# Moving two dense tiles of a delta head from one stage's head to another stage's tail

## The chip, the cores and the metric

One program runs on one core of a Trainium2 chip. The metric is the device time of one execution in microseconds (us), lower is better. The core has five engines with queues of their own: TensorE (PE; its weight loads are shown apart as PEld), VectorE (DVE), ScalarE (ACT), GpSimd (POOL) and SyncE (SP, which here only starts transfers).

## What is computed

Three blocks of a language model on 512 tokens of width 1024, in fp32. The change lies in the first, a mix of a state space part (Mamba-2) and a gated delta rule part:

```python
h = rmsnorm(x, norm_mix_w)
proj = h @ w_in
(ssm_z, ssm_xbc, ssm_dt, gdn_qkv, gdn_z, gdn_a, gdn_b, gate_ssm, gate_gdn) = split(proj)
y_ssm = mamba2_mixer(ssm_z, ssm_xbc, ssm_dt, ...)   # conv, chunked scan, * silu(z), norm
y_gdn = gdn_mixer(gdn_qkv, gdn_z, gdn_a, gdn_b, ...) # conv + silu, 8 heads, delta scan
merged = sigmoid(gate_ssm) * (y_ssm @ w_proj_ssm) + sigmoid(gate_gdn) * (y_gdn @ w_proj_gdn)
x = x + merged @ w_out
```

In `gdn_mixer` the 3072 columns of `gdn_qkv` pass a causal depthwise convolution of four taps and a silu, and are then query, key and value of eight heads of width 128. Each head normalises query and key, solves a unit triangular system in each chunk and runs a scan over chunks.

## The kernel before, in words

**Dense tiles.** Every weight matrix is cut into tiles of 128 output columns. A tile with eight blocks of 128 input rows is computed in four pieces (`("dense", name, j, c)`, two blocks each). A block takes three matmuls of 128x128 by 128x512 (L1054, L1055, L1056), since each fp32 number is split in two rounded parts; a tile is thus 24 matmuls. SP fetches the tile's weights (a panel, 512 KB) into one of three buffers W, ScalarE rounds them into one of four buffers R (L2518), GpSimd forms the rest in four steps (L2910). These `split` steps stand on every engine's queue two panels ahead of the tile that uses them. Two PSUM banks take turns for dense tiles.

**Queues.** Each engine runs its list strictly in order and waits on semaphores. The lists come from `order()`, at build time. Two calls of its planner `weave` matter here: one for the state space stage, one for the delta stage. `weave` gets chains of steps and lists of dense tiles ("fills"), and follows four engines in time with given durations per step (`SEG`). A chain step that is ready goes first; TensorE takes a piece of a dense tile when no chain step is ready, and the next tile as soon as what it depends on (`room`, `AFTER`) and its bank are free. On the other engines steps are ranked by the length of what follows them, and steps that empty a dense bank (`conv`, `sz`, `gate` and others) get 40 us on top. The delta stage is planned for itself, behind the last step of the state space stage on each queue.

**State space stage, tail.** Per group F of 128 columns: dense tile s_z F, then `sz` (ScalarE L2623, VectorE L1882), `sy` (TensorE L1187 and L1190, VectorE L1888 and L1891). After the last four F comes a normalisation: `sn1` (ScalarE square, L2627), `sn1p` (TensorE sums, L1065), `sn2` (VectorE, a root by small steps), `sn2p` (TensorE spreads it, L1072), `sn3` (four VectorE multiplications, L1906) and `pair` (ScalarE L2548 and VectorE L1720 split the result in two parts).

**Delta stage.** g_qkv is tiled so that channel j of the convolution `("conv", "qkv", j)` reads g_qkv tile 8 (j mod 3) + j div 3: head h has channels 3h, 3h+1, 3h+2. `conv` is one ScalarE step (L2564) and three VectorE steps (L1764); `conv2` is ScalarE L2571 and VectorE L1771. Head 2 keeps its channels in tiles 59, 60 and 61 of SBUF, and the same tiles hold masks and the z product of the state space stage until its last F. Two chains run, heads 0, 2, 4, 6 and heads 1, 3, 5, 7. A head begins with `hq` (eight transposes, L1088), which for head 0 waits for the last `sn3`, because it transposes into the bank (4) that `sn3` reads:

```python
w.wait_ge(*CV.dve.at("out", "qkv", 3 * h + 1))
if h == 0:
    w.wait_ge(*SS.dve.at("yn", 7))
transpose4(bank[q.Y], t(q.k)).then_inc(*GD.pe.up("kt", h))
```

Then come `hg` (a row product L1084, VectorE L1969), `hn` (normalisation, ends with L1960), `hnp` (transposes), `hn2` (ScalarE L2658), `hb` (VectorE L1979), `hu` (L1094), an inversion (`i0`, `il`, `ix`, `ip`, `it`, `iq`, `im`, `iu`, `in_`: L1102 or corners L1208 on TensorE, L2637 on ScalarE, L1926 or L1944 on VectorE), a scan over four chunks (`hs1` to `hs3`), and an end with dense tile g_z. The fills are first the remaining g_qkv tiles, a head's three tiles waiting for the head three before it, and then gate_s, p_ssm (eight each), gate_g (eight) and p_gdn (eight half tiles, which need heads 0 to 3 done). In the order before, a pair of heads covers twelve such tiles, the last pair ten; the last four p_gdn half tiles stand between the steps of head 7's inversion.

Of the kernel before, what the change touches and what calls it, by code (L numbers as in the profile page):

```python
# [192 lines left out]
XORD = (8, 9, 10, 11, 0, 1, 2, 3, 4, 5, 6, 7)  # L193
# [75 lines left out]
for f in range(3):  # L269
    PAIR[f"hid{f}"] = (tuple(FS[j % 4] for j in range(NFF)), tuple(range(16, 60, 2)), tuple(range(17, 60, 2)))  # L270
FFN = (("ff_in", 0, "ff_in", 22, 1), ("f1g", 0, "f1u", 0, 4), ("f2g", 0, "f2u", 0, 6))
CONV = {
    "xbc": ("ssm_conv_w", XS, 12, lambda j: ("s_xbc", j), lambda j: ("xbc", XORD[XORD.index(j) - 2]) if XORD.index(j) >= 2 else None),
    "qkv": ("gdn_conv_w", tuple(x for h in range(8) for x in QKV[h % 3]), 24, lambda j: ("g_qkv", 8 * (j % 3) + j // 3),
            lambda j: ("qkv", j - 2) if j >= 2 else ("xbc", 6 + j)),
}
# [6 lines left out]
def rm_bank(q, hh, i):  # L283
# [8 lines left out]
    pair="s.63 v.75", hq="p.86", hqs="s1.2", hn="v6.9", hnp="p.43", hn2="s.6", hg="p.23 v1.38 s1.23", hb="p.23 v1.5",  # L292
# [16 lines left out]
def tiles(name, j, *after):  # L309
    return [("dense", name, j, c) for c in range(-(-WTS[name][1] // CH))] + list(after)  # L310


def opens(name, j):
# [47 lines left out]
    "sa": lambda qb, *u: [("sc", m, qb - 1) + u for m in range(2 if u[0] == "d" else 1)] if qb else [("an3",) + u] + [("fr", u[1]), ("frq", u[1])] * (u[0] == "f"),  # L361
    "sb": lambda m, qb, *u: [("sa", qb) + u],
    "sc": lambda m, qb, *u: [("sb", m, qb) + u], "sd": lambda qb, *u: [("sc", m, qb) + u for m in range(2 if u[0] == "d" else 1)],
    "conv": lambda which, j: [("conv2",) + CONV[which][4](j)] if CONV[which][4](j) else [],
    "conv2": lambda which, j: [("conv", which, j)], "branch": lambda name, j, gname, gj, x, m: [("gate", gname, gj, x)],
    "part": lambda name, j, gname, gj, x, m: [("gate", gname, gj, x)],
    "do_": lambda f: [("dg", f), ("sd", 3, "d", f)], "ft1": lambda h: [("sd", 3, "f", h)],
# [29 lines left out]
def room(name, j):  # L397

    if name == "s_z":
        return [("sy", j - 1)] if j else []  # L400
    if name == "g_z":
        return [("hs3", j, 3)]
    if name == "pa" and j >= 13:
        return [("s3", j - 13, 7)]
    if name == "g_qkv":
        return [("ho2", j % 8 - 3)] if j % 8 >= 3 else []
    if name == "pa":
        return [("pair", "yr", j % 4 - 2)] if j < 12 and j % 4 >= 2 else []
    if name == "gm" and j >= 8:
        return [("ry3", 2)] if j >= 12 else [("ixs", 3, 7)]  # L410
    if name == "a_out":
        return [("pair", "yr", p) for p in range(4)]
    if name == "qkv2":
        return [("pair", "yr", j % 4 + 2)] if j % 4 < 2 else [("ry3", 2), ("ry3", 3), ("branch", "a_out", 7, "gm", 7, M2[7], None)]
    if name == "gb":
        return [("pair", "yr", j + 2)] if j < 2 else [("do_", j - 2)]
    if name == "p_gdn":
        return [("pair", "ygdn", h) for h in range(4)]
    if name == "b_out":
        return [("pair", "yd", p) for p in range(2)]  # L420
    if name == "b_proj":
        return [("pair", "ydiff", h) for h in range(6)]
    if name == "a_proj":
        return [("pair", "yg", f) for f in range(4)]
    if name == "in3" and 16 <= j < 20:
        return [("gn2", 3)] + ([("pair", "yg", j - 18)] if j >= 18 else [])
    if name == "in3" and j >= 24:
        return [("ft3", j % 8 - 4)] if j % 8 >= 4 else [("pair", "yg", 3)] if j % 8 >= 2 else []
    return []


def weave(chains, *fills):
# [9 lines left out]
    for c in units:  # L442
        before = None
        for u in c:
            for k, s in enumerate(u):
                wants[s] = room(*s[1:3]) if s[0] == "dense" and s[3] == 0 else [u[k - 1]] if k else after(s, before)
            before = u[-1]
    for f in dense:
        for u in f:
            for s in u:  # L450
                if s[0] == "dense":
                    wants[s] = room(*s[1:3]) if s[3] == 0 else []
                else:
                    wants[s] = [[x for x in u if x[0] == "dense"][-1]] + (AFTER[s[0]](*s[1:]) if s[0] in AFTER else [])
# [146 lines left out]
def convs(which, js):  # L601
    out = []
    for n, j in enumerate(js):
        out += tiles(*CONV[which][3](j), ("conv", which, j))
        if n:
            out.append(("conv2", which, js[n - 1]))
    return out + [("conv2", which, js[-1])]
# [12 lines left out]
def gdn_head(h):  # L620
    out = [("hq", h), ("hqs", h), ("hg", h), ("hn", h), ("hnp", h), ("hn2", h), ("hb", h), ("hu", h)]
    out += inversion(("g", h), 3) + [("hk", h)]
    for c in range(4):
        out += ([("hs1", h, c)] if c else []) + [("hs2", h, c), ("hs3", h, c), ("ho", h, c)]
    return out + [("hon", h), tiles("g_z", h, ("hz", h)), ("hos", h), ("ho2", h)]
# [72 lines left out]
def gated(name, gname, g0, x, m=None, gates=True):  # L698
    out = []
    for j in range(8):  # L700
        if gates:
            out += tiles(gname, g0 + j, ("gate", gname, g0 + j, x[j]))
        out += tiles(name, j, ("branch", name, j, gname, g0 + j, x[j], m and m[j]))
    return out
# [15 lines left out]
def order():  # L720
    O = [("begin",), ("ada0",), ("halves",)]
# [6 lines left out]
    def channel(g):  # L728
        out = []
        for F in range(4 * g, 4 * g + 4):  # L730
            after = [(k, F + 1, hh) for k in ("ch", "che") for hh in range(2)] if F % 4 < 3 else []
            out += ([(k, F, hh) for k in ("ch", "che") for hh in range(2)] if F % 4 == 0 else []) + [("cm", F, 0), ("cm", F, 1), tiles("s_z", F, ("sz", F))]
            out += after + [("sy", F)] + ([("xd", F + 4)] if g == 0 else [])
        return out

    def normed(g):
        out = []
        for f in range(4):
            out += [("sn1", g, f), ("sn1p", g, f)]
        return (out + [("sn2", g), ("sn2p", g)] + [("sn3", 4 * g + f) for f in range(4)]  # L740
                + [("pair", "yssm", 4 * g + f) for f in range(4)])

    chain = [tiles("small", 0)] + [("sums", n) for n in range(5)]
    for g in range(2):
# [1 line left out]
        for c in range(3):  # L746
            chain += [("st0", g, c), ("st", g, c)]
        chain += channel(g)
    O += weave([chain, normed(0) + normed(1)], convs("xbc", XORD) + convs("qkv", range(6)))

    rest = gated("p_ssm", "gate_s", 0, M1)
    rest += [s for j in range(8) for s in tiles("gate_g", j, ("gate", "gate_g", j, GG[j]))]
    rest += [s for j in range(8) for s in tiles("p_gdn", j, ("part", "p_gdn", j, "gate_g", j, GG[j], M1[j]))]
    heads = [[s for h in range(a, 8, 2) for s in gdn_head(h)] for a in range(2)]
    O += weave(heads + [[("pair", "ygdn", h) for h in range(4)]], sum([convs("qkv", range(3 * h, 3 * h + 3)) for h in range(2, 8)], []), rest)
    O += [("pair", "ygdn2", h) for h in range(4)]
    O += wide(followed("p_gdn2", "gate_g", 0, GG, M1, "m1") + residual("w_out", 1))
    O += ffn(0, "ff_dn", 2, True)
# [11 lines left out]
    rest = [s for j in range(8) for s in tiles("gm", j, ("gate", "gm", j, M2[j]))] + sum(gates[:4], [])  # L770
# [19 lines left out]
    rest = gated("a_proj", "in3", 0, M3) + gates  # L790
# [77 lines left out]


ORDER = [x if x[0] in ALONE else (ALL, x) for x in order()]  # L870
ON_PE = [s for e, s in ORDER if "p" in e]
TURN = turns(ON_PE)
# [2272 lines left out]
```

## Time and profile before

| | |
|---|---|
| time, median of 3 runs | 3094.06 us (3093.57 to 3095.58) |
| profiled execution, from first to last instruction | 3089.4 us |
| time around that span (median less span) | 4.7 us |
| TensorE busy | 2977.7 us, 96% |
| VectorE, ScalarE, GpSimd busy | 1605.5, 1078.7, 1412.1 us |
| state space stage's last `sy` ends on TensorE | 234.06 us |
| delta stage on TensorE | 246.47 to 724.48 us |
| granted TensorE clock, mean | 0.988 |

The profile shows one execution. Times in its rows are microseconds from the start of the span, durations in us, and "PE" before a line number is TensorE's matmul row. A wait is written as idle time of an engine with the instruction that ended it. `PEclk`, in the rows of stretches the third number from the end, is the clock that was granted to TensorE, 1.00 for 2.4 GHz and 0.50 for 1.2 GHz. The execution's own time is not shown apart from the span, so the time around it is taken from the median.

### The profile page before, as it was taken

Reading aid. Unit: us, or ns where it says so; the run is one execution under the profiler, and the core shown is the slowest. Engines: PE = TensorE matmul, PEld = TensorE weight load, DVE = VectorE, ACT = ScalarE, POOL = GpSimd, SP = SyncE. Lnnn points to the kernel's source line nnn. Section 1 sums busy time; section 2 is a strip of 40 time slices with the busy share of each in tenths; the row PEclk is TensorE's granted clock in tenths of the full one; section 3 lists DMA queues with packets and bytes.
Section 4 is the critical chain, followed back from the end, with each engine's and each line's share of the span. In section 5 each row is a group of like instructions: output and inputs, shape, how many; then the busy total and the mean of one; then the engine's idle time right before and its main releaser. Section 6 shows DMA issues by size and latency. Waiting matters only on the chain.

```text
span 3089.4 us, 42486 instructions
## 1 busy us (share of the span) xinstructions
PE 2977.7 (96%) x16912; PEld 2385.2 (77%) x16912; DVE 1605.5 (52%) x3295; ACT 1078.7 (35%) x1781; POOL 1412.1 (46%) x1817
## 2 busy tenths in 40 slices
PE   6998999999999999999999999999899999999999
PEld 5777777787888887767877778888776768788887
DVE  5766567566566416559744453330466773433310
ACT  4443333333322223323324433222354553332221
POOL 3553344344556544314334364555543334655554
PEclk9999999999999999999999999999999999999999
DMA  3211112112344432102112222333321112232232
GB/s 123 83 55 60 57 55 69 55 56 82 117 149 144 129 96 66 36 21 69 36 48 75 69 82 96 96 94 101 101 69 61 58 59 81 84 96 96 97 103 88
DMA packets 72358, 248.02 MB, mean 80 GB/s; under 512 B 8160, under 2 KB 8544, under 8 KB 72032
## 3 DMA queue, kind: packets, MB, share of 16 engines
q1 hardware_dynamic: 72160, 245.30, 24.8%
q8 instruction: 134, 2.20, 0.3%
q14 instruction: 64, 0.52, 0.1%
HBM read 243.18 MB, written 2.10 MB: 79 GB/s over the span
## 4 chain that ended last, share of the span: by engine, by line
PE 84%; DVE 12%; ACT 2%; issue 1%; POOL 1%; DMA 0%; SPq 0%; DVEq 0%; ACTq 0%; POOLq 0%
PE bank L1054 23%; PE bank L1056 22%; PE bank L1055 22%; PE bank L1088 3%; PE bank L1102 3%; PE bank L1533 1%; PE bank L1065 1%; PE bank L1551 1%; DVE sm L1617 1%; DVE sm L1619 1%; PE bank L1542 1%; PE bank L1372 1%; DVE sm L1621 1%; POOL t L2943 1%; DVE t L1764 1%
## 5 line engine op out<-in xcount | busy, mean ns | idle before, releaser
L2910 POOL TENSOR_TENSOR R<-W,R 128x256 fp32r<-128x256 f32 x1715 | 1287.9, 784 | 1540.5 <-ACT R L2518 1540.5
L1054 PE MATMUL bank<-u,R 128*128 128x512 f32 (+1 forms) x3440 | 1393.9, 405 | 27.2 <-DVE u L1720 8.3
L1056 PE MATMUL bank<-u,R 128*128 128x512 f32 (+1 forms) x3440 | 1348.8, 392 | 0.0
L1055 PE MATMUL bank<-u,R 128*128 128x512 f32 (+1 forms) x3440 | 1347.8, 392 | 0.0
L1054 PEld LDWEIGHTS bank<-u,R 128*128 128x128 f32 (+1 forms) x3440 | 649.2, 189 | 182.5 <-issue 15.9
L1056 PEld LDWEIGHTS bank<-u,R 128*128 128x128 f32 (+1 forms) x3440 | 648.6, 189 | 142.4 <-issue 0.4
L1055 PEld LDWEIGHTS bank<-u,R 128*128 128x128 f32 (+1 forms) x3440 | 650.3, 189 | 127.5 <-issue 4.8
L2518 ACT ACTIVATE R<-W 128x1024 fp32r<-128x1024 f32 (+2 forms) x454 | 452.3, 1002 | 143.3 <-PE bank L1056 136.8
L2548 ACT ACTIVATE u<-t 128x512 fp32r<-128x512 f32 x126 | 78.3, 630 | 322.9 <-DVE t L1742 249.1
L1753 DVE SCALAR_TENSOR_TENSOR X<-bank,X 128x512 f32<-128x512 f32 x32 | 22.1, 692 | 260.2 <-PE bank L1056 260.2
L1720 DVE TENSOR_TENSOR u<-t,u 128x512 fp32r<-128x512 f32 x126 | 97.3, 782 | 100.5 <-ACT u L2548 99.8
L1088 PE MATMUL bank<-CN,t 128*128 128x128 f32 x816 | 122.5, 281 | 20.5 <-DVE t L2044 5.4
L1728 DVE TENSOR_TENSOR t<-bank,t 128x512 f32<-128x512 f32 x66 | 45.5, 689 | 172.5 <-PE bank L1056 164.4
L1088 PEld LDWEIGHTS bank<-CN,t 128*128 128x128 f32 x816 | 91.5, 142 | 45.5 <-DVE t L2300 8.0
L2555 ACT ACTIVATE t<-t 128x512 f32<-128x512 f32 x66 | 41.7, 632 | 240.8 <-DVE t L1728 240.8
L1742 DVE TENSOR_TENSOR t<-t,bank 128x512 f32<-128x512 f32 x66 | 45.4, 688 | 128.2 <-PE bank L1056 126.3
L1102 PEld LDWEIGHTS bank<-t,t 64*64 64x64 f32 x2560 | 83.3, 134 | 30.6 <-issue 25.4
L1102 PE MATMUL bank<-t,t 64*64 64x64 f32 x2560 | 98.3, 222 | 0.1
L1764 DVE SCALAR_TENSOR_TENSOR t<-bank,sm,t 128x511 f32<-128x511 f32 (+2 forms) x108 | 80.6, 747 | 24.6 <-ACT t L2564 22.0
L2524 ACT ACTIVATE t<-X 128x512 f32<-128x512 f32 x48 | 29.8, 623 | 152.3 <-DVE X L1753 73.9
L2819 ACT ACTIVATE t<-t,sm 128x128 f32<-128x128 f32 (+3 forms) x96 | 62.0, 647 | 43.4 <-DVE sm L2318 42.8
L1733 DVE SCALAR_TENSOR_TENSOR t<-t,t 128x512 f32<-128x512 f32 x66 | 52.7, 798 | 37.7 <-ACT t L2555 37.7
(389 smaller groups left out, 2748.4 us busy)
## 6 DMA issues: line engine op xcount, KB each, us to landing
W<-in_in SPq DMA_DIRECT2D x48, 512.0 KB, 3.3
W<-in_ff_in SPq DMA_DIRECT2D x44, 512.0 KB, 3.3
W<-in_g_qkv SPq DMA_DIRECT2D x24, 512.0 KB, 3.3
W<-in_ada SPq DMA_DIRECT2D x24, 512.0 KB, 3.3
W<-in_f1g SPq DMA_DIRECT2D x22, 512.0 KB, 3.3
W<-in_f1u SPq DMA_DIRECT2D x22, 512.0 KB, 3.2
W<-in_f2g SPq DMA_DIRECT2D x22, 512.0 KB, 3.2
W<-in_f2u SPq DMA_DIRECT2D x22, 512.0 KB, 3.3
```

The source lines that it names most:

```text
L1054: e.matmul(b[0:cols, :], wh, hi, start=(k == 0), stop=False)
L1055: e.matmul(b[0:cols, :], wh, lo, start=False, stop=False)
L1056: i = e.matmul(b[0:cols, :], wl, hi, start=False, stop=(k == KT - 1))
L1088: i = e.transpose(b[:, m * 128:m * 128 + 128], x[:, m * 128:m * 128 + 128], C("ident"))
L1102: i = e.matmul(b[g, s], l[g, s], x[g, s], start=True, stop=True)
L1720: e.tensor_tensor(r(lo[k]), t(src[k]), r(hi[k]).bitcast(F32), SUB).then_inc(*PR.dve.up("lo", tag, k))
L1733: e.scalar_tensor_tensor(out=s, in0=t(FT[j % 2]), scalar=1.0, in1=s, op0=ADD, op1=MUL).then_inc(*FF.dve.up("s", f, j))
L1764: e.scalar_tensor_tensor(out=c[:, s:512], in0=b[:, 0:512 - s], scalar=half(wname, (3 - s) * nt + gj), in1=c[:, s:512], op0=MUL, op1=ADD).t ...
L2518: e.activation(R[q % NH][:, 0:n], W[p % NW][:, 0:n], ACT.Copy).then_inc(*PN.act.up("hi", key))
L2548: e.activation(r(hi[k]), t(src[k]), ACT.Copy).then_inc(*PR.act.up("hi", tag, k))
L2819: e.activation(ex, ex, ACT.Exp, bias=c[:, 0:1], scale=small[q.nw][:, 32 + 2 * qb + m:33 + 2 * qb + m], accum_out=c[:, 1:2]).then_inc(*AT.a ...
L2910: i = e.tensor_tensor(R[q % NH][:, 1024 + a:1024 + b], W[p % NW][:, a:b], R[q % NH][:, a:b].bitcast(F32), SUB)
```

## The change

Channels 6 and 7 of the qkv convolution, head 2's first two (g_qkv tiles 2 and 10), are planned in the state space stage's call of `weave` and no longer in the delta stage's. Two entries hold them back there: the two dense tiles depend on `sz` 7, the step that reads the last z tile's bank, and their `conv` steps on `sy` 7. Channel 8 stays in the delta stage, and everything that is computed stays as it is.

```diff
--- before.py
+++ after.py
@@ -361,7 +361,7 @@
     "sa": lambda qb, *u: [("sc", m, qb - 1) + u for m in range(2 if u[0] == "d" else 1)] if qb else [("an3",) + u] + [("fr", u[1]), ("frq", u[1])] * (u[0] == "f"),
     "sb": lambda m, qb, *u: [("sa", qb) + u],
     "sc": lambda m, qb, *u: [("sb", m, qb) + u], "sd": lambda qb, *u: [("sc", m, qb) + u for m in range(2 if u[0] == "d" else 1)],
-    "conv": lambda which, j: [("conv2",) + CONV[which][4](j)] if CONV[which][4](j) else [],
+    "conv": lambda which, j: [("sy", 7)] * (which == "qkv" and j in (6, 7)) + ([("conv2",) + CONV[which][4](j)] if CONV[which][4](j) else []),
     "conv2": lambda which, j: [("conv", which, j)], "branch": lambda name, j, gname, gj, x, m: [("gate", gname, gj, x)],
     "part": lambda name, j, gname, gj, x, m: [("gate", gname, gj, x)],
     "do_": lambda f: [("dg", f), ("sd", 3, "d", f)], "ft1": lambda h: [("sd", 3, "f", h)],
@@ -403,7 +403,7 @@
     if name == "pa" and j >= 13:
         return [("s3", j - 13, 7)]
     if name == "g_qkv":
-        return [("ho2", j % 8 - 3)] if j % 8 >= 3 else []
+        return [("ho2", j % 8 - 3)] if j % 8 >= 3 else [("sz", 7)] * (j in (2, 10))
     if name == "pa":
         return [("pair", "yr", j % 4 - 2)] if j < 12 and j % 4 >= 2 else []
     if name == "gm" and j >= 8:
@@ -746,13 +746,13 @@
         for c in range(3):
             chain += [("st0", g, c), ("st", g, c)]
         chain += channel(g)
-    O += weave([chain, normed(0) + normed(1)], convs("xbc", XORD) + convs("qkv", range(6)))
+    O += weave([chain, normed(0) + normed(1)], convs("xbc", XORD) + convs("qkv", range(8)))
 
     rest = gated("p_ssm", "gate_s", 0, M1)
     rest += [s for j in range(8) for s in tiles("gate_g", j, ("gate", "gate_g", j, GG[j]))]
     rest += [s for j in range(8) for s in tiles("p_gdn", j, ("part", "p_gdn", j, "gate_g", j, GG[j], M1[j]))]
     heads = [[s for h in range(a, 8, 2) for s in gdn_head(h)] for a in range(2)]
-    O += weave(heads + [[("pair", "ygdn", h) for h in range(4)]], sum([convs("qkv", range(3 * h, 3 * h + 3)) for h in range(2, 8)], []), rest)
+    O += weave(heads + [[("pair", "ygdn", h) for h in range(4)]], convs("qkv", range(8, 9)) + sum([convs("qkv", range(3 * h, 3 * h + 3)) for h in range(3, 8)], []), rest)
     O += [("pair", "ygdn2", h) for h in range(4)]
     O += wide(followed("p_gdn2", "gate_g", 0, GG, M1, "m1") + residual("w_out", 1))
     O += ffn(0, "ff_dn", 2, True)
```

## Rows read from the trace of the kernel before

**Rows 1.** The page: span, and busy time of each engine.

```profile
span 3089.4 us, 42486 instructions
...
PE 2977.7 (96%) x16912; PEld 2385.2 (77%) x16912; DVE 1605.5 (52%) x3295; ACT 1078.7 (35%) x1781; POOL 1412.1 (46%) x1817
```

**Rows 2.** Stretches, busy time by engine: start and end, length, then busy us (instructions), clock, DMA.

```profile
234.06:246.47 12.41, 3.02 (x17) 2.75 (x17) 7.98 (x25) 2.54 (x5) 0.00 (x0) 0.66 0.00 0
246.47:251.65 5.18, 5.18 (x17) 4.40 (x17) 1.43 (x3) 2.60 (x4) 2.79 (x4) 0.50 0.02 3
251.65:270.00 18.35, 17.78 (x88) 14.80 (x87) 16.26 (x32) 6.35 (x9) 9.39 (x13) 1.00 0.27 86
246.47:724.48 478.01, 463.51 (x3480) 376.23 (x3480) 305.97 (x648) 165.52 (x320) 191.69 (x236) 0.99 0.18 58
677.19:698.41 21.22, 21.22 (x214) 16.55 (x213) 13.27 (x25) 6.19 (x12) 11.89 (x14) 1.00 0.20 61
```

**Rows 3.** Chain that ended last, 228 to 252: start us, us, what.

```profile
228.50 0.23 PE bank L1055
...
232.15 0.23 PE bank L1056
...
234.10 0.76 DVE t L1888
...
236.29 1.07 PE bank L1065 x8
...
240.35 1.99 PE bank L1072 x8
242.36 0.76 DVE t L1906
...
246.47 1.97 PE bank L1088 x8
248.44 0.43 PE bank L1054
...
251.00 0.44 PE bank L1084
251.46 0.70 DVE t L1969
```

**Rows 4.** Timeline 225 to 300: start us, us, engine, line, operation [idle before, releaser].

```profile
226.96 1.04 ACT L2518 ACTIVATE R<-W 128x1024 fp32r<-128x1024 f32 x1
...
228.08 2.81 POOL L2910 TENSOR_TENSOR R<-W,R 128x256 fp32r<-128x256 f32 x4 [4.58 <-ACT R L2518]
```

**Rows 5.** Timeline 255 to 275, three engines.

```profile
255.77 0.69 ACT L2564 ACTIVATE t<-bank,sm 128x512 f32<-128x512 f32 x1 [0.79 <-PE bank L1056]
...
259.82 4.54 DVE L1764 SCALAR_TENSOR_TENSOR t<-bank,sm,t 128x511 f32<-128x511 f32 x6
...
261.81 0.59 ACT L2658 ACTIVATE t<-bank 128x512 f32<-128x512 f32 x1
...
262.19 0.50 PE L1054 MATMUL bank<-u,R 128*128 128x512 f32 x1 [0.57 <-DVE t L1764]
...
264.28 0.68 DVE L1979 TENSOR_TENSOR t<-t,bank 128x512 f32<-128x512 f32 x1
...
271.19 1.47 PE L1088 MATMUL bank<-CN,t 128*128 128x128 f32 x12
```

**Rows 6.** PE's waits in the delta stage: us in total, times, longest.

```profile
PE bank L1054 <- DVE t L1764: 3.6, 3, 1.5
```

**Rows 7.** Timeline, tail of the delta stage: one link, then PE's rows.

```profile
660.14 0.68 PE L1102 MATMUL bank<-t,t 64*64 64x64 f32 x16
...
660.87 0.69 DVE L1926 TENSOR_TENSOR t<-t,bank 128x512 f32<-128x512 f32 x1 [2.57 <-PE bank L1102]
...
679.39 0.51 PE L1102 MATMUL bank<-t,t 64*64 64x64 f32 x10
...
698.41 0.68 PE L1208 MATMUL bank<-t,t 64*64 64x64 f32 x8
```

## The prediction

> **What bounds the kernel now.** I read the page first: TensorE is busy 96% of the span, no other engine more than 52% [rows 1]. So a change in the order of the work can only win what TensorE idles, or what it does at a lower clock, at the place that the change touches. Next the stretches of time around that place [rows 2]. The state space stage ends its TensorE work on the last product (`sy` 7) at 234.06, and the delta stage's first instruction (`hq` 0, eight transposes) starts at 246.47. In these 12.41 us TensorE has 3.02 us of work, so 9.4 us are idle; the granted clock has sunk, and the next 5.18 us run wholly at 0.50, the 1.2 GHz level. The chain of waits says what the idle time is [rows 3]: VectorE combines `sy` 7, ScalarE squares, TensorE sums (L1065), VectorE takes a root from 237.4 to 240.3, TensorE spreads it (L1072), VectorE multiplies four tiles (L1906), and only then do the transposes get their turn, because `hq` 0 waits for the last of these four. Behind them in TensorE's queue stands tile 2 of g_qkv, which needs none of that.
>
> In the delta stage, 246.47 to 724.48, TensorE idles 478.0 - 463.5 = 14.5 us in all [rows 2], spread over many small waits, of which the convolution's L1764 causes 3.6 us in three [rows 6]. Here two chains of heads alternate with dense tiles that fill their waits.
>
> **What the edit moves.** g_qkv tiles 2 and 10 (query and key of head 2, channels 6 and 7 of the convolution) with their convolutions leave the head of the delta stage for the end of the state space stage, from 234.06 on. `sz` 7 ends on VectorE before `sy` 7 is combined at 234.10, so the hold costs TensorE nothing. No matmul, transfer or byte is added. The order of panels stays s_z 7, g_qkv 2, 10, 18, gate_s 0, so SP's queue only moves earlier. The panel of tile 10 is the one that GpSimd splits from 228.08 to 230.9 [rows 4], so both are ready at 234.06. The next splits (1.04 us on ScalarE, 2.8 on GpSimd each) have both engines free: GpSimd is idle in the whole gap [rows 2]. Cost of all this: nothing, covered by the gap; without cover one split would delay a later tile by up to 3.9 us.
>
> **Terms of the sum.**
> A. The two tiles. In the chain seventeen matmuls of a dense tile lie between 228.50 and 232.38, 0.228 us each [rows 3]. Two tiles are 2 x 24 x 0.228 = 10.9 us that the delta stage no longer holds.
> B. The clock. If the gap is filled, the transposes and the first dense work run at full clock. The eight transposes took 1.97 us [rows 3], twelve of them at full clock 1.47, so eight about 1.0 [rows 5]: 1.0 won. From 248.44 to 251.46 seven big matmuls take 0.43 each instead of 0.23 [rows 3], 1.4 won, and one more before the clock is back about 0.1. B = 2.5.
> C. Head 0 starts later. The two moved tiles now share TensorE with the tail's own two small jobs. Pieces of six matmuls (1.37 us) can't be interrupted: the sum L1065, ready at 236.29, starts after two pieces at 236.79, 0.5 late. The spread L1072, ready at about 240.85, starts behind the first piece of tile 10 at about 241.96, but takes 1.0 instead of 1.97, so it ends at 243.0, 0.7 later than now. Tile 2 is through at 240.6; ScalarE's first step takes 0.69 and VectorE's three steps about 2.3 (six take 4.54) [rows 5], 241.3 to 243.6, and an evacuation goes first in the planner's ranking, so I count it ahead of the four L1906. These, with two `pair` steps between them, took from 242.36 to the transposes' start at 246.47, 4.1 us [rows 3]; they now end at 247.7. TensorE's own queue is through with both tiles at 234.06 + 10.9 + 1.07 + 1.0 = 247.1, so VectorE decides: start at 247.7, C = -1.2. Its lower bound is 0.6 late (TensorE's queue alone), its upper bound, if the second convolution also stands ahead, is the rival below.
> D. New idle time. The planner gives dense tiles to TensorE as early as they fit, so the idle slots of the heads stay filled from the tiles behind (gate_s, p_ssm, gate_g), and what is missing is the last fill: four half tiles of p_gdn, eight pieces. They now run in the 21.2 us from 677.2 to 698.4, in which TensorE is wholly busy [rows 2], and between them stands head 7's inversion, from its third squaring at 679.39 to its last corner at 698.41, 19.0 us [rows 7]. One link there is a TensorE job of 0.68 and a VectorE step of 0.69, 660.14 to 661.56, so 1.42 [rows 7]. I count seven such links and a similar one over ScalarE: 11 us if nothing is in the way, 12 to 13 with head 6's jobs between. So without the eight pieces, 10.9 us, this stretch shrinks by only 6 to 7: 4 to 5 us of TensorE become idle. Lower bound 0: if the chains run faster earlier (next term), less fill is used there and more is left here. Upper bound 8, if only 3 us come out of the chain. I take 4.2, nearer to the counted links than to either end.
> E. VectorE is relieved in the head of the stage. It is busy 16.3 of 18.35 us there [rows 2], and head 0 waits behind six convolution steps, 259.82 to 264.36, before L1979 at 264.28; TensorE lost 0.57 at 262.19 for the same reason [rows 5]. These steps are gone from there. On TensorE that is 0.6 at least; I take 0.6, with up to 3 for the chain if the chain counts.
>
> Sum: 10.9 + 2.5 - 1.2 - 4.2 + 0.6 = 8.6 us less. The profiled span is 3089.4; the median of the runs, 3094.06, lies 4.7 above it, which is the time around the span and doesn't change. Span 3080.8, time **3085.5**, 0.28% less. What a measurement of this kernel can tell from no change is 0.2%, 6.2 us.
>
> Of the transposes the Trainium skill (TensorE: Matmul & The Clock Gate, Part 4: PE-mode transpose) says that the full clock doesn't engage for them. By it `hq` 0 would keep its 1.97 us, and the time would be 3086.5. The trace disagrees: twelve in 1.47 us.
>
> **Rivals.**
> 1. The heads' chain sets the delta stage, and fill taken from it is simply idle time. For it: links and pieces are planned to dovetail, and the stage's rounds end with head steps. Against it: only 14.5 of 478 us are idle, and TensorE's jobs there often stand behind a piece. What then counts is the chain of head 0: now its row product L1084 ends at 251.4; later 247.7 + 1.0 + 1.37 + 0.4 = 250.5, 0.9 sooner; and `hb` comes 1.8 sooner (L1979 starts at 264.28; the last step before it, L2658, ends at 262.4 [rows 5]). 2.7 us less: **3091.4**.
> 2. TensorE alone sets it: no new idle time, D = 0. Then 10.9 + 2.5 - 1.2 + 0.6 = 12.8 less: **3081.3**. For it: the 96%; against it: the last fill stands exactly where only two chains are left.
> 3. Slower: head 0 starts late and the stage is paced by its heads. If VectorE's queue has the second convolution ahead of the four L1906, it begins at 247.1 + 0.7 = 247.8, ends at 250.1, and the L1906 at 254.2; the transposes start 7.7 us later, TensorE idles 7 us before them, and as in today's gap the clock falls to 1.2 GHz, so B is lost as well. If the stage then keeps its 478 us, less the 1.8 us that `hb` wins, the time is 3094.1 + 7.7 - 1.8 = **3100.0**. Against it: by the planner's own order the four multiplications are ready (behind L1072) several us before tile 10's last matmul. It decides from a late start of about 5 us on, and only with the heads as the bound; with TensorE as the bound the same late start would still give 3094 or less.
> 4. The edit does not fill the gap, since the planner may put the tiles behind L1072: then nothing before 242 is filled, and the gain is that of rival 1 or less. It is counted there; the planner takes a known dense tile at the first free moment, so I think it unlikely.
>
> **How the numbers follow.** Forecast (6.2 to 11 us less) 0.49; rival 2 (11 to 14) 0.15; rival 1 with rival 4 (0 to 6 less) 0.28; rival 3 and other bad interleavings of a stage that is planned anew 0.08. Faster by over 0.2% is the first two, 0.64. Rival 1 and a small part of rival 3 are within 0.2%: 0.29. Slower: 0.07. The range reaches from rival 2's value with 0.8 for the bound of C, 3080.5, to the upper end of rival 1, 3094.0; outside lie rival 3 and the far ends, under 0.15. The likeliest case's own range is 3083 to 3088.
>
> **What would show it.** Right: the granted clock between 234 and 252 stays near 1.00; dense matmuls stand between 234.1 and 247; the transposes of `hq` 0 start at 247 to 248 and take 1.0 us; the first L1906 starts at 243 to 244. In round four (from about 600) idle time of 3 to 5 us appears before the scan of head 7, in the waits on L1926, L1944 or L2637. The distance from `hq` 0 to the stage's end falls from 478.0 to about 468. Wrong: that distance stays above 474 (rival 1), falls below 465 (rival 2), or the transposes start after 252 (rival 3). Most of all D is weak: it rests on which tiles the planner leaves for the end, and a new order may also cost waits in rounds two and three that nothing in the present trace shows.

## The result and the profile after

The changed kernel takes 3100.65 us (median of 12 executions, 3097.86 to 3115.65) against 3094.06 for the kernel before (12 executions beside it, 3092.99 to 3095.58). The ratio is 1.0029, 95% interval 1.0021 to 1.0037: slower by 0.29%, where 0.28% faster was forecast and 3080.5 to 3094.0 was the range.

The page after, span and busy time by engine, answers to [rows 1]:

```profile
span 3098.6 us, 42487 instructions
...
PE 2984.4 (96%) x16912; PEld 2389.3 (77%) x16912; DVE 1606.6 (52%) x3295; ACT 1077.8 (35%) x1781; POOL 1411.1 (46%) x1817
```

The stretches after, for [rows 2] (length, then busy us with instructions by engine, clock, DMA): from the end of `sy` 7 to `hq` 0, the half-rate part behind it, the delta stage, its last round, and a hole inside that round.

```profile
233.92:252.50 18.58, 13.04 (x64) 10.29 (x63) 14.90 (x32) 6.42 (x11) 5.87 (x8) 0.96 0.18 58
252.50:257.81 5.31, 5.30 (x17) 4.53 (x18) 2.67 (x5) 2.61 (x4) 3.37 (x4) 0.50 0.00 0
252.50:729.07 476.57, 455.63 (x3433) 368.27 (x3433) 301.93 (x642) 161.00 (x314) 185.52 (x228) 0.99 0.17 56
614.74:729.07 114.33, 103.66 (x801) 82.09 (x801) 81.20 (x172) 37.00 (x79) 35.80 (x42) 0.97 0.12 38
645.00:655.00 10.00, 5.11 (x40) 4.01 (x39) 8.29 (x25) 4.09 (x8) 0.00 (x0) 0.77 0.00 0
```

The gap is filled, as forecast: TensorE has 13.04 us of work in it instead of 3.02. But the gap itself is 6.2 us longer, and behind it 5.3 us run at 0.50, as 5.2 us did before. The stage holds 10.9 us less work and is only 1.4 us shorter (476.57 against 478.01): TensorE is busy 7.88 us less, not 10.9, since more of its work runs at half rate, and it idles 20.9 us instead of 14.5.

The timeline after around `hq` 0, VectorE with the rows of ScalarE, GpSimd and TensorE that it meets, answers to [rows 3]:

```profile
237.36 2.83 POOL L2910 TENSOR_TENSOR R<-W,R 128x256 fp32r<-128x256 f32 x4 [0.40 <-ACT R L2518]
...
237.69 0.43 DVE L1633 TENSOR_SCALAR sm<-sm 128x4 f32<-128x4 f32 x1
238.16 0.67 DVE L1635 TENSOR_SCALAR sm<-sm 128x4 int32<-128x4 int32 x1
238.85 0.66 DVE L1637 TENSOR_SCALAR sm<-sm 128x4 int32<-128x4 int32 x1
239.55 0.66 DVE L1640 TENSOR_TENSOR sm<-sm 128x4 f32<-128x4 f32 x1
240.24 0.17 DVE L1642 SCALAR_TENSOR_TENSOR sm<-sm 128x4 f32<-128x4 f32 x1
...
240.38 0.69 ACT L2564 ACTIVATE t<-bank,sm 128x512 f32<-128x512 f32 x1 [3.10 <-PE bank L1056]
...
242.06 2.31 DVE L1764 SCALAR_TENSOR_TENSOR t<-bank,sm,t 128x511 f32<-128x511 f32 x3
...
242.19 1.11 PE L1072 MATMUL bank<-CR,sr 128*128 128x128 f32 x8 [0.49 <-DVE sr L1657]
...
244.29 0.68 DVE L1771 SCALAR_TENSOR_TENSOR t<-t,t 128x512 f32<-128x512 f32 x1
...
244.89 1.40 DVE L1906 SCALAR_TENSOR_TENSOR t<-t,PC,bank 128x512 f32<-128x512 f32 x2
...
246.33 0.69 DVE L1720 TENSOR_TENSOR u<-t,u 128x512 fp32r<-128x512 f32 x1
...
247.50 0.69 ACT L2564 ACTIVATE t<-bank,sm 128x512 f32<-128x512 f32 x1 [1.20 <-PE bank L1056]
...
248.22 2.32 DVE L1764 SCALAR_TENSOR_TENSOR t<-bank,sm,t 128x511 f32<-128x511 f32 x3 [1.20 <-ACT t L2564]
...
250.45 0.74 DVE L1906 SCALAR_TENSOR_TENSOR t<-t,PC,bank 128x512 f32<-128x512 f32 x1
...
251.11 0.68 DVE L1771 SCALAR_TENSOR_TENSOR t<-t,t 128x512 f32<-128x512 f32 x1
...
251.71 0.74 DVE L1906 SCALAR_TENSOR_TENSOR t<-t,PC,bank 128x512 f32<-128x512 f32 x1
...
252.50 1.97 PE L1088 MATMUL bank<-CN,t 128*128 128x128 f32 x8 [5.04 <-DVE t L1906]
```

VectorE's order is the cause of the late start. Only two of the four L1906 run at 244.9. Then the queue has the convolution of channel 7, whose dense tile ends at 247.5, so VectorE waits 1.2 us for it, works 2.3, and the last two L1906 come at 250.45 and 251.71. TensorE idles 5.04 us, and its clock goes down: the trace's record of the granted clock has 0.50 from 251.0 to 257.8.

TensorE's waits in the last round, after (us in total, times, longest):

```profile
PE bank L1088 <- DVE t L1960: 4.9, 1, 4.9
PE bank L1054 <- DVE t L2054: 2.3, 1, 2.3
```

The first is the hole at 645 to 655: `hnp` 7 waits for the normalisation `hn` 7, and no dense tile is left that may run, because p_gdn 0 needs the pairs of heads 0 to 3 and the planner had used up gate_g before them. Rounds one to three (a round is the work of one pair of heads) hold the same number of dense matmuls in both kernels, 306, 354 and 336; the last holds 300 before and 252 after, two tiles less. The first matmuls behind the hole are at 0.50 too: the clock record has 6.8 us of it from 650.3.

### The profile page after: what moved, and what is told of

The parts are those of the page before. It is cut to its first block, busy times and chain, and to the rows that moved or that the text cites. A ratio compares the mean times of both kernels' runs of the same rounds, so it can differ in the third digit from the quotient of the medians.

```text
span 3098.6 us, 42487 instructions
## 1 busy us (share of the span) xinstructions
PE 2984.4 (96%) x16912; PEld 2389.3 (77%) x16912; DVE 1606.6 (52%) x3295; ACT 1077.8 (35%) x1781; POOL 1411.1 (46%) x1817
## 4 chain that ended last, share of the span: by engine, by line
PE 84%; DVE 12%; ACT 2%; issue 1%; POOL 1%; DMA 0%; SPq 0%; DVEq 0%; ACTq 0%
PE bank L1054 23%; PE bank L1056 22%; PE bank L1055 22%; PE bank L1088 3%; PE bank L1102 3%; PE bank L1533 1%; PE bank L1065 1%; PE bank L1551 1%; DVE sm L1617 1%; PE bank L1542 1%; DVE sm L1619 1%; DVE t L2163 1%; DVE t L1764 1%; DVE sm L1621 1%; DVE sm L2161 1%
```

## The experiments

Ten kernels ran. The first table is read from the traces (one profiled execution each): "start" is the time from `sy` 7 on VectorE (L1888) to the last L1906, which lets `hq` 0 go; rounds one to four end with the second head's last L2044 of each pair and, the fourth, with the stage's last step L2054; "to end" is start plus rounds; then TensorE's idle time in the rounds, and how much of them the granted clock was at 0.50. In e6 the last L1906 stands inside round one, so it has no row; its distance from `sy` 7 to the stage's last step is 494.3.

| us | start | round 1 | 2 | 3 | 4 | to end | idle | at 0.50 |
|---|---|---|---|---|---|---|---|---|
| before | 11.57 | 116.06 | 124.17 | 122.33 | 114.83 | 488.96 | 13.9 | 6.0 |
| after | 17.95 | 116.09 | 124.14 | 122.05 | 113.62 | 493.86 | 20.3 | 12.9 |
| e1_tail_by_hand | 12.51 | 122.96 | 124.17 | 122.11 | 113.59 | 495.33 | 25.8 | 17.1 |
| e2_one_tile | 13.26 | 115.29 | 128.87 | 122.03 | 112.05 | 491.51 | 17.4 | 11.1 |
| e3_hold_gates | 17.96 | 116.06 | 124.49 | 118.79 | 111.66 | 488.96 | 14.8 | 13.2 |
| e4_less_fill | 11.58 | 109.07 | 121.51 | 122.39 | 114.84 | 479.38 | 18.0 | 7.1 |
| e5_tail_and_gates | 12.52 | 118.80 | 124.23 | 119.06 | 113.29 | 487.89 | 18.8 | 10.2 |
| e7_late | 17.38 | 115.50 | 124.10 | 122.36 | 114.87 | 494.20 | 14.1 | 4.3 |
| e8_late_two | 13.02 | 115.26 | 124.14 | 122.28 | 114.82 | 489.53 | | 3.9 |
| e9_late_sixteen | 23.19 | 115.50 | 124.14 | 122.34 | 114.82 | 500.00 | | 4.4 |
| e10_late_tiny | 11.96 | 116.02 | 124.13 | 122.39 | 114.85 | 489.35 | | 5.6 |

The second table has the times. Many of these kernels, and never the kernel before in the 74 executions beside them, have executions with a mean clock of 0.979 to 0.982 that take 11 to 20 us more (e6: 5); they are counted apart, and the median of the others stands beside. What the traces show of them stands at the end.

| | median, us | ratio [95%] | at 0.979 to 0.982 | median of the others |
|---|---|---|---|---|
| before (four sets) | 3093.16 to 3094.35 | | 0 of 74 | |
| after | 3100.65 | 1.0029 [1.0021, 1.0037] | 2 of 12 | 3100.4 |
| e1 | 3103.14 | 1.0038 [1.0023, 1.0053] | 2 of 6 | 3102.3 |
| e2 | 3097.42 | 1.0014 [1.0002, 1.0026] | 2 of 12 | 3096.8 |
| e3 | 3093.14 | 0.9999 [0.9990, 1.0007] | 0 of 11 | 3093.1 |
| e4 | 3098.01 | 1.0005 [0.9993, 1.0016] | 7 of 11 | 3086.8 |
| e5 | 3102.70 | 1.0023 [1.0008, 1.0038] | 6 of 12 | 3092.7 |
| e6 | 3107.40 | 1.0041 [1.0029, 1.0053] | 3 of 5 | 3103.2 |
| e7 | 3115.57 | 1.0053 [1.0035, 1.0070] | 4 of 6 | 3101.0 |
| e8 | 3110.42 | 1.0049 [1.0033, 1.0064] | 5 of 6 | 3095.9 |
| e9 | 3113.27 | 1.0064 [1.0045, 1.0082] | 3 of 6 | 3106.2 |
| e10 | 3093.64 | 1.0007 [0.9994, 1.0020] | 2 of 12 | 3093.0 |

**e1: the late start undone by hand.** The changed kernel, with VectorE's and ScalarE's order in the tail rewritten:

```diff
+def by_hand(O):
+    q, y = [("conv", "qkv", 6), ("conv", "qkv", 7)], [("pair", "yssm", f) for f in range(4, 8)]
+    c = [("conv2", "qkv", j) for j in (5, 6, 7)]
+    n = [("sn3", f) for f in range(4, 8)]
+    v = [("v", s) for s in q[:1] + n + c[:2] + q[1:] + [("hg", 0), ("hn", 0)] + y + c[2:]]
+    s = [("s", s) for s in q[:1] + c[:1] + y + c[1:2] + q[1:] + c[2:]]
...
+    O = by_hand(O)
```

> Edit: the changed kernel, but on VectorE and ScalarE the steps around the state space stage's end are put in another order by hand: the four L1906 stand ahead of the second moved convolution, and the last splits (L1720) behind the normalisation of head 0. Theory 1 (the late start of head 0 is passed on in full): the transposes of head 0 start near 247.3 instead of 252.5, its L1969 near 250.5 instead of 257.5, the clock stays up, and the time falls by 6 to 7 us against the changed kernel, to about 3094. Rival (a late start is absorbed by the waits of the delta stage, and the loss comes from the hole in round four and the clock later on): less than 2 us of it reach the end, 3099 to 3101.

`hq` 0 starts 5.4 us sooner, but round one is 6.9 us longer. TensorE's waits in round one of e1 (line numbers are 15 higher than in the kernel after):

```profile
PE bank L1069 <- DVE t L1779: 5.4, 1, 5.4
PE bank L1103 <- DVE t L2059: 2.5, 1, 2.5
PE bank L1103 <- DVE t L1975: 1.3, 1, 1.3
```

L1779 is the convolution: channel 8's stood behind the four `pair` steps that I had moved behind `hn` 0, and p_ssm 0 needed its bank. A new wait took the place of the old one, so this run doesn't give the price of the late start. The time, 3102.3 at the usual clock, lies above both expectations.

**e2: one tile moved, not two.**

```diff
-    O += weave([chain, normed(0) + normed(1)], convs("xbc", XORD) + convs("qkv", range(8)))
+    O += weave([chain, normed(0) + normed(1)], convs("xbc", XORD) + convs("qkv", range(7)))
...
-... convs("qkv", range(8, 9)) + sum([...
+... convs("qkv", range(7, 9)) + sum([...
```

> Edit: only the first of the two tiles (channel 6) moves, the second stays at the head of the delta stage. Theory 1 (the heads pace the stage, filled or not): the tail is filled by 5.5 us, one convolution stands among the four L1906, head 0 starts 1 to 3 us later than before, and the time is 3094 to 3097. Rival (TensorE paces it): 5.5 us of work less in the delta stage, minus the late start, 3089 to 3092.

The start is only 1.7 us later than before and the last round 2.8 shorter, but round two is 4.7 longer: the plan of that round came out differently with a wait of 2.7 us on L2027 (0.8 in round three of before). Half of the change costs about 2.5 us, the whole 6.4 (medians at the usual clock). The time is in the range of the first expectation, but not for its reason: only 1.7 us of the loss is the start, and the last round did get shorter.

**e3: the fill kept for the hole.** The changed kernel, with one entry more in `room`, so that tiles of gate_g are left when head 7 begins:

```diff
+    if name == "gate_g" and j == 5:
+        return [("hq", 6)]
```

> Edit: the changed kernel, with three gate_g tiles held back in the planner until head 6 begins, so that round three has two dense tiles less and round four has its ten again. Theory 1 (heads pace the rounds): round three is as long as with twelve tiles (122 us), the hole of round four is gone but the round is 115.5 us as before, and the time stays within 2 us of the changed kernel, 3099 to 3102. Rival (TensorE paces the rounds): round three shortens by about 10 us to 112, round four has no hole, and the time falls to 3091.

The hole is gone. The stage of e3, and its last round (stretches):

```profile
250.50:721.50 471.00, 456.17 (x3432) 370.47 (x3432) 301.45 (x642) 159.62 (x312) 185.21 (x228) 0.99 0.18 56
609.84:721.50 111.66, 108.39 (x833) 87.84 (x833) 77.20 (x169) 36.47 (x77) 38.45 (x46) 1.00 0.16 46
```

Idle time in the stage is 14.8 us, about that of before (13.9), and the last round's clock is 1.00 instead of 0.97. The stage is 4.9 us shorter than in the kernel after, and the median 7.5 us lower: with the late start still in it, the change is now worth nothing, neither way. Neither expectation holds: round three is 118.8 us, between 122 and 112, and the time is nearer to the second's 3091. Start and round one are those of the kernel after, so the 4.9 us come from where the fill stands. They are idle time (5.5 us less in the rounds), not clock: the time at 0.50 is 13.2 us in the rounds as against 12.9, since two stretches of 3.4 us stand elsewhere (from 362.6 and from 601.6) in place of the one behind the hole.

**e4: fill taken away from the kernel before.** Nothing is moved; gate_s is computed with one of its three matmuls left out (64 matmuls, 14.6 us), so that part of the product is missing.

```diff
-                    e.matmul(b[0:cols, :], wh, lo, start=False, stop=False)
+                    if name != "gate_s":
+                        e.matmul(b[0:cols, :], wh, lo, start=False, stop=False)
```

> Edit: the kernel before, in its own order, with the second of the three matmuls of each block left out in the eight gate_s tiles (part of the product is left out): 64 matmuls of 0.228 us, 14.6 us of TensorE work less, all in rounds one and two, nothing else changed. Theory 1 (heads pace the rounds): rounds one and two shorten by less than 4 us together and TensorE idles more, time 3090 to 3094. Rival (TensorE paces them): 12 to 14.6 us less, 3080 to 3082.

The stage ends 9.6 us sooner for 14.6 us of work: 66% is paid, 34% turns into waits (idle 18.0 instead of 13.9) and clock. Neither "TensorE alone" nor "the heads' chain alone" sets the stage, and 3086.8 lies between the two expectations. In the four executions at the usual clock the time falls by 7.5 us; the median doesn't show it, since it lies among the seven others.

**e5: both repairs together,** with channel 8's convolution put ahead of the `pair` steps:

```diff
+    v = [("v", s) for s in q[:1] + n + c[:2] + y[:1] + q[1:] + [("hg", 0), ("hn", 0), ("conv", "qkv", 8)] + y[1:] + c[2:]]
...
+    if name == "gate_g" and j == 5:
+        return [("hq", 6)]
```

> The changed kernel with both repairs at once: gate_g tile 5 is held until hq 6, as in e3, and in the tail the four L1906 stand right behind the first convolution step of channel 6 on VectorE, with the split of the second group's results (pair) behind hn 0 and the convolution of channel 8, so that nothing of head 0 waits for them. Theory (the late start of head 0 and the missing fill of round four are two separate costs that add): hq 0 starts at 247 to 248 at full clock, 5 us sooner than in e3; the distance from sy 7 on VectorE to the stage's end, 489.0 in e3, falls to 484 to 485; time 3087 to 3090. Rival (the stage gives an early start back in its first two rounds, as e1 did, where round one grew from 116.1 to 123.0): that distance stays at 488 or above and the time is 3092 to 3096.

The rival's numbers hold, almost exactly. The start is 5.4 us sooner than in e3, and the stage's end only 1.1. Of the 4.3 us given back, 2.7 go in round one, 0.3 in round three and 1.6 in round four; the last are half rate, not a wait: there TensorE is busy 110.0 us for 108.4, with 3.4 us at 0.50 that e3 doesn't have in that round. TensorE's waits in round one of e5 (lines 17 higher than before):

```profile
PE bank L1105 <- DVE t L2061: 2.5, 1, 2.5
PE bank L1105 <- DVE t L1977: 1.9, 1, 1.9
PE bank L1071 <- DVE t L1781: 1.8, 1, 1.8
```

The 2.5 stands in e3 too. The 1.9 (`hnp` 0 on `hn` 0) and the 1.8 (a bank on a convolution) are new there, and all three are waits on VectorE. The six steps of the two moved convolutions and their two `conv2` are about 6 us of VectorE wherever they stand: ahead of `hq` 0 they delay the transposes, behind it they delay `hn` 0 and channel 8.

**e6: the gap removed at its other end.** From the kernel before, no tile moved: the second normalisation gets bank 5, `hq` 0 waits for `yn` 3 only, and the second group's steps from the fourth `sn1` on (the last square and sum, the root, the multiplications and the pairs) are planned in the delta stage.

```diff
-                    w.wait_ge(*SS.dve.at("yn", 7))
+                    w.wait_ge(*SS.dve.at("yn", 3))
...
-    O += weave([chain, normed(0) + normed(1)], convs("xbc", XORD) + convs("qkv", range(6)))
+    O += weave([chain, normed(0) + normed(1)[:6]], convs("xbc", XORD) + convs("qkv", range(6)))
```

> From the kernel before, without moving any tile: the idle stretch of 9.4 us is taken away at its other end. The second group's normalisation uses bank 5 in place of bank 4, so that hq 0 waits for the first group's L1906 only; the sums, the root, the four L1906 and the pairs of the second group are planned as a third chain inside the delta stage, hg 1 waits for them, and p_ssm waits for the pairs. hq 0 should start at 235 to 237 instead of 246.5, at full clock. Theory (an idle stretch before the stage counts in full when nothing is put in its place, since TensorE keeps all its fill): the distance from sy 7 to the stage's end falls from 489.0 to 479 to 482, time 3084 to 3088. Rival (the heads' chain sets the stage and the new small chain delays VectorE's steps of head 0 and 1): the distance stays above 485 and the time above 3090.

The theory is wrong on all counts; the rival's bounds hold (494.3 from `sy` 7 to the stage's end, 3103.2 at the usual clock), but not for its reason alone. The state space stage, planned anew without its last chain, reached `sy` 7 5.4 us later (239.5 instead of 234.1), `hq` 0 started at 241.0, VectorE had the root of the second group among head 0's steps, 17.1 us from 280.9 on were at 0.50, and the stage ended 10.7 us later (733.8). Two plans were changed at once here, so it says nothing on the worth of the gap alone, only that taking the wait away doesn't bring it in.

**e7, e8, e9, e10: a late start and nothing else.** The kernel before, with VectorE steps that leave the data as they are ahead of the first L1906 of the second group, eight (e7), two (e8) or sixteen (e9), or two on four columns (e10). Every queue keeps its order.

```diff
+                for again in range(8 if F == 4 else 0):
+                    e.scalar_tensor_tensor(out=x, in0=x, scalar=1.0, in1=x, op0=MUL, op1=MAX).then_inc(*SS.dve.up())
+                    w.wait_ge(*SS.dve.now())
```

> From the kernel before, with nothing else changed: eight additional VectorE steps of about 0.7 us each, that leave the data as they are (the larger of x and x), stand ahead of the first of the second group's four L1906. So hq 0 starts 5.5 to 6.5 us later, with the same order on every queue behind it. It measures the price of a late start by itself. Theory (the price is paid in full, as the sum of the prediction had it, since the order of the stage is fixed): the stage keeps its 477 to 478 us, time 3099 to 3101. Rival (the stage absorbs most of it in its waits): stage 473 or less, time 3094 to 3096. The granted clock behind the stage should be as in the kernel before; if it is lower, the clock follows the shift and not the change's own order.

> The kernel before with two (in place of e7's eight) additional VectorE steps ahead of the second group's L1906: hq 0 starts 1.4 to 1.5 us later, everything behind it in the same order. Theory (a late start is passed on one to one, and the granted clock behind the stage depends on where in time the later stages fall, not on the changed kernel's order): the distance from sy 7 to the stage's end is 490 to 491, and the time is 3095 to 3096 where the clock stays as in the kernel before; executions with 13 to 15 us more and a mean clock near 0.980 may occur. Rival (the clock behind the stage is a matter of the size of the delay, idle time in which the clock falls for good): with 1.5 us no execution has a mean clock below 0.985.

> The same with sixteen steps, about 11.6 us later. Theory: the stage passes all of it on, the distance from sy 7 to its end is 500 to 501, the time 3106 to 3108 in executions with the clock of the kernel before, and up to 15 us more where the clock falls in a later stage. Rival (a longer idle time lets the stage catch up, since ScalarE, GpSimd and the transfers run ahead): the distance stays below 498.

> The kernel before with two additional VectorE steps on 128x4 elements (0.17 us each) ahead of the second group's L1906. Everything behind it moves by at most 0.4 us, and the order is the same on every queue. It asks what brings on the executions with a mean clock near 0.981, of which the kernel before has none and e7 to e9 have 12 in 18. Theory (the start time of the delta stage decides, by whole microseconds): with 0.4 us the kernel behaves as before, all executions at 0.985 or above, median 3093 to 3095. Rival (any change of the timing or of the instruction lists brings them on, since the stretch of small matmuls some 1100 us later stands at an edge): at least one in four executions is at 0.979 to 0.983 and takes 3107 to 3112.

The start moves by 5.81, 1.45, 11.62 and 0.39 us, the stage's end by 5.24, 0.57, 11.04 and 0.39. The theories of e7 and e9 hold. In this order of work a late start is passed on but for 0.9 us at most, whatever its size (so e8 passes on only 0.57 of 1.45, just short of its theory's 490 us); the 0.6 to 0.9 us that three of them keep go with the clock, which is back sooner behind the start (3.9 to 4.4 us at 0.50 in the rounds, not 6.0). In executions at the usual clock (two, one and three) e7 takes 3101.0, e8 3095.9, e9 3106.2: 7, 3 and 13 us more than before, so about 2 us of each are not in the stage's own delay. The medians of e7 and e8 lie among the low executions, which the first expectation didn't have at all. The rival of e8, that so short a delay leaves no execution below 0.985, is refuted: five of six are.

## Why the prediction was wrong, step by step

From VectorE's step on `sy` 7 to the stage's last step L2054, before takes 489.0 us and after 493.9, which is 4.9 us more (by TensorE's marks, 12.41 + 478.01 against 18.58 + 476.57, it is 4.7). By the forecast it would have been 8.6 less. Two of the three signs of being wrong came: `hq` 0 started behind 252 (rival 3), and the distance from it to the stage's end stayed above 474 (rival 1). The terms:

- **A, the two tiles, 10.9 us.** Right as work: the last round holds 48 dense matmuls less, and TensorE has them in the gap.
- **B, the clock, 2.5 us won.** Nothing was won. The gap was full until 247.46, but for 0.5 us, and at full clock, but the 5.04 us of waiting behind it took the clock down again; the transposes took 1.97, and 5.3 us ran at 0.50, as before.
- **C, the late start, 1.2 us.** It was 6.4. This is the step that failed first. I counted one convolution ahead of the four L1906; the queue had both ahead of the last two, with two `conv2` that the sum didn't have, and 1.2 us of waiting for tile 10. The forecast argued against this that the four are "ready (behind L1072) several us before tile 10's last matmul". Ready they were, but the order of the queue decides, and it had only two of them there. The third rival had this mechanism, its length (6.4 instead of 7.7) and the fall of the clock, and I gave it and all other bad plans together 0.08. e7 shows the price by itself: 5.8 later, 5.2 lost.
- **D, new idle time, 4.2 us, and E, 0.6 won.** Together 3.6; measured 6.4 (20.9 against 14.5), within D's bound of 8, but in another place than I had it. Not the end of head 7's inversion lost its fill but the wait for `hn` 7, where one hole of 4.9 us was deep enough to bring the clock down. Half rate there cost another 3.0 us, for which the sum had no term. The 3.0 is what is missing from the work (TensorE's busy time fell by 7.9 instead of 10.9); the clock record bears it out with 6.9 us more at 0.50 in the rounds, half of which is 3.4. e3 shows that the idle part was a matter of which tiles were left: one entry more closes the hole and takes 5.5 of the 6.4 us away. The half rate it does not win back (13.2 us at 0.50 in the rounds); what brings the stretches elsewhere on was not looked into.
- **E by itself.** VectorE has less to do in round one (66.1 us instead of 69.8), but it brought nothing. The wait of 0.57 us that was to go is still there, 0.55, behind another convolution, and L1979 starts 17.7 us behind `hq` 0, where it was 17.8; VectorE now waits 2.0 us for TensorE ahead of it. And the steps were not taken away but put on the same queue ahead of those that head 0 waits for. The rows of after (timeline):

```profile
268.24 0.50 PE L1054 MATMUL bank<-u,R 128*128 128x512 f32 x1 [0.55 <-DVE t L1764]
...
270.18 0.69 DVE L1979 TENSOR_TENSOR t<-t,bank 128x512 f32<-128x512 f32 x1 [2.00 <-PE bank L1084]
```

The balance: 6.4 (start) - 10.9 (work) + 3.0 (half rate) + 6.4 (idle) = 4.9. It closes by its making, since the 3.0 is a remainder; what is measured apart is the start, the idle time and the clock record. The medians differ by 6.6; the 1.7 us left are a difference of medians and one trace each, and no trace gives them a place. Behind the stage, with the same 12360 matmuls, TensorE is busy 3.7 us longer in the profiled execution of after, so the clock has a part in it. The forecast also took 4.7 us for the time around the span; it is 1.7 to 1.9 in every execution that lists both, and the rest was that the profiled execution of before was a quick one (about 3091.2). Last, the lower end of the range was worked out with 0.8 for the bound of C where its own bound of 0.6 us gives 0.6, so 3080.7 and not 3080.5; this changes nothing.

Of the rivals, the first (the heads' chain) and the second (TensorE alone) are both half right: e4 pays 66% of removed work. The fourth, a gap that isn't filled, did not happen. The third came, with half its condition: it was meant to need the heads as the only bound and at least 5 us; e7 to e9 show that the stage passes a late start on, but for under 1 us, as long as its order is fixed. That its 3100.0 lies within 0.7 us of the measured 3100.65 is in part luck. It had the stage at 476.2 because the heads would pace it; the stage takes 476.6, but as 10.9 us of work less, 3.0 of half rate and 6.4 of idle time more, and e3, with the same late start, has it at 471.0.

What is left open is whether any placing makes the change pay. e3 (no difference) and e5 (3092.7 at the usual clock, but half of its executions at 3107 to 3110) don't beat the kernel before.

## What to carry to other kernels

Before work is moved into a gap of one engine, follow all its steps on the other engines: here TensorE's 10.9 us fitted, and 6 us of VectorE that came with them stood ahead of the very steps that ended the gap. Where a planner or a fixed queue order decides, forecast the order on every queue of the stretch, not only what is ready when. And fill that is spent early in a greedy plan is missing at the one wait without a substitute (here 4.9 us of idle time, with 6.8 us at half rate behind it); it can be kept for that place by a dependency.

## What the runs showed of the hardware

**The clock can fall with TensorE never idle.** In the profiled executions of e7, e8 and e9 (mean clock 0.979 to 0.981) there is one stretch of 37.5 us at 0.50 that the kernel before doesn't have, always over the same instructions, some 1100 us behind the edit. The stretch in e7, with the one ahead of it (stretches):

```profile
1309.00:1345.00 36.00, 36.00 (x281) 27.05 (x280) 12.46 (x49) 6.49 (x15) 5.55 (x8) 1.00 0.09 30
1345.00:1382.50 37.50, 37.50 (x175) 25.90 (x176) 11.71 (x37) 7.81 (x19) 2.79 (x4) 0.50 0.02 6
```

and the same work in the kernel before:

```profile
1301.63:1337.60 35.97, 35.97 (x281) 27.04 (x279) 12.44 (x48) 6.50 (x15) 5.57 (x8) 1.00 0.09 31
1337.60:1358.70 21.10, 21.10 (x175) 15.09 (x176) 11.49 (x37) 7.83 (x19) 1.65 (x3) 1.00 0.00 1
```

TensorE is busy without a break in both, and takes 37.5 instead of 21.1 us. (Busy time is the profile's reckoning, in which the ends of matmuls are modelled; it lists no wait of TensorE between 1340 and 1385 in e7.) The timeline of e8 where its clock falls, a run of small matmuls (64 and 128 columns) without a dense piece between them; the kernel before has the same run at 1.00:

```profile
1336.83 0.29 PE L1479 MATMUL bank<-t,t 128*64 128x64 f32 x4
1337.04 0.48 PE L1463 MATMUL bank<-t,t 64*128 64x128 f32 x2
1337.37 0.38 PE L1464 MATMUL bank<-t,t 64*128 64x128 f32 x2
1337.68 0.69 PE L1473 MATMUL bank<-t,t 128*128 128x64 f32 x2
1338.30 0.48 PE L1476 MATMUL bank<-t,t 128*64 128x64 f32 x4
1338.57 0.43 PE L1479 MATMUL bank<-t,t 128*64 128x64 f32 x4
```

The Trainium skill (TensorE: Matmul & The Clock Gate, HAM oscillation — how this bites in real kernels) gives avoiding longer idle gaps of TensorE as the rule for keeping the full clock. The rows at 252.50 and 645 agree with it; the stretch of e7 shows that here the absence of gaps was not enough.

What brings it on isn't settled. It isn't where the work lies in time: in its one trace, e8 reaches 1318 us within 0.2 us of the kernel before and has the stretch, and 5 of its 6 executions are low. It isn't the size of the shift either: 0.4 us (e10) gave 2 low executions of 12, where both expectations, none or at least one in four, miss (the second not by more than chance allows). Whether the low executions of the other kernels are of this kind was not seen: their profiled executions were at 0.984 to 0.988. Only e6's was low (0.981), and it doesn't have this stretch; its half rate is spread over several places, 48 us ahead of the stage's end against 24 in the kernel before. For a study of fractions of a per cent it means that a median can jump by 12 to 15 us through an edit that costs 1.5.

**VectorE's small steps take longer while GpSimd works.** In the timeline after, four steps of the root on 128x4 elements take 0.43, 0.67, 0.66 and 0.66 us while GpSimd's four split pieces run (237.36 to 240.2), and 0.17 from 240.24 on. In e2, where GpSimd is done at 238.2, the same steps (timeline):

```profile
239.12 0.17 DVE L1635 TENSOR_SCALAR sm<-sm 128x4 int32<-128x4 int32 x1
239.33 0.17 DVE L1637 TENSOR_SCALAR sm<-sm 128x4 int32<-128x4 int32 x1
239.53 0.17 DVE L1640 TENSOR_TENSOR sm<-sm 128x4 f32<-128x4 f32 x1
```

The root takes 4.65 us instead of the 2.9 of the kernel before; e3 and e5, with the split at the same place, have the same long steps. The Trainium skill (SBUF — State Buffer, Who interferes with whom) says that VectorE and GpSimd share one pair of ports as an exclusive lock, which in VectorE's modes of two ports whoever issues first holds for the whole instruction. The length fits that: each step takes about as long as one split piece, 2.83 / 4 = 0.7 us. That these steps run in such a mode no row shows. The forecast had costed the earlier splits at nothing because GpSimd was idle in the gap. They cost 1.75 us of VectorE in the chain that ends the gap. Most of it was hidden this time: the spread L1072 started at 242.19 instead of the forecast 241.96, and VectorE waited for tile 10 further on.
